# A recurrent (mLSTM) stage rebuilt one chunk ahead of itself, with its gate rows brought by broadcast DMA

## What is computed

```python
def step(carry, inp):
    C, n, m = carry
    qb, kb, vb, li, lf = inp
    bcum = jnp.cumsum(lf, axis=-1)
    dmat = bcum[..., :, None] - bcum[..., None, :] + li[..., None, :]
    dmat = jnp.where(causal, dmat, -jnp.inf)
    inter = bcum + m[..., None]
    m_t = jnp.maximum(inter, jnp.max(dmat, axis=-1))
    w_intra = jnp.exp(dmat - m_t[..., None])
    w_inter = jnp.exp(inter - m_t)
    s_qk = jnp.einsum('bhtd,bhsd->bhts', qb, kb) * w_intra
    num = (w_inter[..., None] * jnp.einsum('bhvd,bhtd->bhtv', C, qb)
           + jnp.einsum('bhts,bhsv->bhtv', s_qk, vb))
    den = w_inter * jnp.einsum('bhd,bhtd->bht', n, qb) + jnp.sum(s_qk, axis=-1)
    h = num / jnp.maximum(jnp.abs(den), jnp.exp(-m_t))[..., None]
    ...
    C_new = decay[..., None, None] * C + jnp.einsum('bhs,bhsv,bhsd->bhvd', w_state, vb, kb)
    ...
```

## Time and profile before

| what | value |
|---|---|
| median of 3 runs | 2396.52 us (2394.82 to 2397.51) |
| the profiled execution | 2397.14 us, its span 2395.4 us |
| TensorE busy | 2280.5 us (95% of the span) |
| VectorE, ScalarE, GpSimd busy | 1256.0, 681.5, 108.7 us |
| mean granted TensorE clock | 0.982 of full |
| recurrent stage on TensorE | first instruction of chunk 0 at 236.00 us, of chunk 7 at 366.11 us |

### The profile page before, as it was taken

The page is one execution under the profiler, slowest core; times in us unless marked ns, Lnnn a source line. Parts: engine busy times, 40 slices in busy tenths (PEclk is TensorE's granted clock), DMA queues, the critical chain, the costliest instruction groups (busy, mean ns, idle before and its releaser), DMA issues. The chain is left out here.

```text
span 2395.4 us, 28953 instructions
## 1 busy us (share of the span) xinstructions
PE 2280.5 (95%) x10838; PEld 1895.0 (79%) x10838; DVE 1256.0 (52%) x2161; ACT 681.5 (28%) x1328; POOL 108.7 (5%) x156
## 2 busy tenths in 40 slices
PE   4999899999999999999998988999999999999997
PEld 3788678787888888888887867987788888888886
DVE  6334443568555455455566546756834433433447
ACT  2300333344112112113145227814411211211221
POOL 0000001110000000000021000011100000000003
PEclk9999899999999999999999998999999999999999
DMA  6433223212332232232221101111211201210211
GB/s 249 124 105 120 92 64 113 71 36 71 91 121 78 89 114 79 87 114 88 82 85 64 50 30 45 37 36 53 71 40 48 70 31 39 70 38 32 70 36 70
DMA packets 48354, 179.77 MB, mean 75 GB/s; under 512 B 6112, under 2 KB 6256, under 8 KB 47760
## 3 DMA queue, kind: packets, MB, share of 16 engines
q1 hardware_dynamic: 42768, 161.50, 21.5%
q0 software_dynamic: 4752, 16.93, 2.0%
q10 hardware_dynamic: 752, 0.22, 0.0%
HBM read 170.24 MB, written 8.39 MB: 75 GB/s over the span
## 5 line engine op out<-in xcount | busy, mean ns | idle before, releaser
L1441 PE MATMUL ps<-uhi,whi 128*128 128x512 f32 x1152 | 452.2, 393 | 15.2 <-DVE ulo L931 7.3
L1442 PE MATMUL ps<-ulo,whi 128*128 128x512 f32 x1152 | 450.3, 391 | 0.0
L1443 PE MATMUL ps<-uhi,wlo 128*128 128x512 f32 x1152 | 450.2, 391 | 0.0
L1441 PE MATMUL ps<-whi,hhi 128*128 128x512 f32 x1024 | 401.1, 392 | 5.2 <-DVE resid L1237 5.2
L1442 PE MATMUL ps<-wlo,hhi 128*128 128x512 f32 x1024 | 399.6, 390 | 0.0
L1443 PE MATMUL ps<-whi,hlo 128*128 128x512 f32 x1024 | 399.5, 390 | 0.0
L1237 DVE TENSOR_TENSOR resid<-ps,resid 128x512 f32<-128x512 f32 x256 | 176.4, 691 | 355.7 <-PE ps L1443 340.0
L733 ACT ACTIVATE h_whole<-ps 128x512 f32<-128x512 f32 x128 | 76.4, 597 | 835.3 <-PE ps L1443 835.3
L1441 PE MATMUL ps<-whi,uhi 128*128 128x512 f32 x704 | 282.7, 402 | 12.4 <-DVE wlo L900 9.0
L900 DVE TENSOR_TENSOR wlo<-stage,whi 128x1024 fp32r<-128x1024 f32 x180 | 219.8, 1225 | 124.4 <-ACT whi L572 124.3
L1443 PE MATMUL ps<-whi,ulo 128*128 128x512 f32 x704 | 277.0, 394 | 0.0
(11 more groups left out here) (214 smaller groups left out, 2149.6 us busy)
## 6 DMA issues: line engine op xcount, KB each, us to landing
stage<-in_stream SPq DMA_DIRECT2D x276, 512.0 KB, 3.6
aux<-in_early SPq DMA_DIRECT2D x2, 2048.0 KB, 10.7
early_place<-in_early SPq DMA_DIRECT2D x2, 2048.0 KB, 19.9
resid<-in_xt SPq DMA_DIRECT2D x8, 512.0 KB, 24.8
resid<-in_x POOLq DMA_DIRECT2D x8, 512.0 KB, 6.7
resid_dram<-resid POOLq DMA_DIRECT2D x8, 512.0 KB, 3.0
resid<-resid_dram POOLq DMA_DIRECT2D x8, 512.0 KB, 3.5
out<-resid SPq DMA_DIRECT2D x8, 512.0 KB, 2.6
```

Source lines behind the costliest of these rows:

```text
L1441: pe.matmul(dst, left_hi, right_hi, start=start, stop=False)
L1442: pe.matmul(dst, left_hi, right_lo, start=False, stop=False)
L1443: return pe.matmul(dst, left_lo, right_hi, start=False, stop=stop)
```

## The change

- The rows of `negm` and `winter` are no longer made by TensorE. GpSimd writes both arrays to DRAM once, then for each chunk issues two DMAs on its own queue that read four rows of 512 bytes and write them to all 128 partitions: `winter` rows into `decay_rows`, `negm` rows straight into `dmat` (256 KB each). ScalarE takes the exp in place from SBUF.
- Scores and transposed keys of chunk c+1 are made at the start of chunk c; those of chunk 0 inside the v pass. `ktok` has two buffers. The weighted scores are written over the keys in `qk`.
- The numerators are made in two pairs of heads, both pairs in banks X+2 and X+3. VectorE copies each pair to `qk` (`take_raw`), so squares and scaling on ScalarE read and write SBUF. Chunk 0 leaves out the products with the zero state.
- The state products use bank M, one head at a time, each waiting for the update of the head before.
- The o projection of chunk c stands in chunk c (parts 0 and 1, then 2, then 3, with the state products between), no longer in chunk c+1.
- On GpSimd the preparation of chunk c+1 stands ahead of the power of chunk c.
- The heads lie in another order in `qk`, so `transpose_tile` reads them `by_pairs`.

```diff
@@ gpsimd
-            for c in range(T):
-
+            pool.wait_ge(gate_v, 11)
+            pool.wait_ge(gate_e, 7)
+            for w, src in enumerate((negm, winter)):
+                pool.dma_start(rows_dram[w], src[:]).then_inc(rows_out, 16)
+            pool.wait_ge(rows_out, 32)
+            def chunk_rows(w, c, dst, landed):
+                src = rows_dram[w].rearrange("(h t) n -> t h n", t=T)[c]
+                pool.dma_start(dst, src.partition_broadcast(P)).then_inc(landed, 16)
+            def prepare(c):
+                if c:
+                    pool.wait_ge(q_weighted, c)
+                chunk_rows(1, c, decay_rows[:].rearrange("p (h n) -> p h n", h=H), winter_in)
+                if c:
+                    pool.wait_ge(s_ready, c)
+                chunk_rows(0, c, dmat[:], negm_in)
                 pool.wait_ge(d_ready, c + 1)
                 pool.affine_select(out=dmat[:], in_=dmat[:], ...
+            prepare(0)
+            for c in range(T):
+                if c + 1 < T:
+                    prepare(c + 1)
                 pool.wait_ge(ms_ready, c + 1)
                 pool.tensor_tensor(mean, mean, neghalf[:], ALU.pow).then_inc(rms_ready, 1)
@@ scalar
+            act.wait_ge(rows_out, 32)
+            decays(0)
+            keys_by_token(0)
+            splits(18, 19)
             for c in range(T):
+                if c + 1 < T:
+                    decays(c + 1)
+                    keys_by_token(c + 1)
+                if c == 0:
+                    splits(20, 21)
                 for h in range(H):
+                    act.wait_ge(raw_ready, 2 * c + h // 2 + 1)
+                    if H * c + h:
+                        act.wait_ge(ss_ready, H * c + h)
+                    act.activation(squares[:], head_out(c, h), ACT.Square,
                                    accum_out=sumsq[:, h:h + 1]).then_inc(ss_ready, 1)
                 act.wait_ge(f_ready, c + 1)
                 for h in range(H):
+                    act.activation(head_out(c, h), head_out(c, h), ACT.Copy,
                                    scale=factor[:, h:h + 1]).then_inc(hs_ready, 1)
+                evac_o(0, c)
@@ vector
+            def take_raw(c, pair):
+                if c:
+                    v.wait_ge(f_ready, c)
+                v.wait_ge(num_done, H * c + 2 * pair + 2)
+                v.tensor_copy(r[:, 2 * pair:2 * pair + 2], ps[:, X + 2:X + 4, DV])
+                v.tensor_copy(two_heads(c, pair), ps[:, X + 2:X + 4, 0:DV]).then_inc(raw_ready, 1)
             for c in range(T):
+                if c + 1 < T:
+                    weigh(c + 1)
+                take_raw(c, 0)
                 if c == 4:
                     take_mod(G_F0)
+                update(c, 0)
+                more = range(2 * (c % 4), 2 * (c % 4) + 2)
+                adas((G_F0, SH_KV)[c // 4], more[0:1] if c else more)
+                if c:
+                    apply_gate(0, c - 1)
+                take_raw(c, 1)
+                update(c, 1)
...
                 v.tensor_scalar(mean, mean, 1.0 / DV, RMS_EPS, ALU.mult, ALU.add).then_inc(ms_ready, 1)
+                update(c, 2)
                 v.wait_ge(rms_ready, c + 1)
                 v.tensor_tensor(factor, mean, r, ALU.mult).then_inc(f_ready, 1)
+                if c == 0:
+                    preps(20, 21)
                 else:
+                    adas((G_F0, SH_KV)[c // 4], more[1:2])
+                update(c, 3)
@@ tensor
             for c in range(T):
+                if c + 1 < T:
+                    scores_and_keys(c + 1)
+                numerators(c, 0)
+                if c == 4:
                     pe.wait_ge(c_updated, H * c)
+                    sum_vector(G_F0)
+                by_token(FIRST["o0"] + c, W_O, c, part=(0, 1))
+                if c == 0:
+                    pe.wait_ge(sum_read, SC_F0 + 1)
+                if c == 4:
+                    pe.wait_ge(sum_read, G_F0 + 1)
+                state(c, 0)
+                numerators(c, 1)
+                state(c, 1)
+                by_token(FIRST["o0"] + c, W_O, c, part=(2,))
+                state(c, 2)
+                by_token(FIRST["o0"] + c, W_O, c, part=(3,))
+                state(c, 3)
+            pe.wait_ge(c_updated, H * (T - 1))
             sum_vector(SH_KV)
-            by_token(FIRST["o0"] + T - 1, W_O, T - 1)
```

More of the change, by code:

```diff
@@ L273, in build @@
         with ExitStack() as a:
+            squares = sb("squares", [P, DV], where=a)
+        with ExitStack() as a:
             rope = sb("rope", [P, T, 2 * ROT], where=a)
@@ L281, in build @@
             dmat = sb("dmat", [P, H, P], where=a)
[L282 to L286, removed]
+            ktok = sb("ktok", [P, 2, H, P], where=a)
+            with ExitStack() as b:
+                gw = sb("gw", [P, K, 8], where=b)
+                gws = sb("gws", [P, K, 16], F32R, where=b)
+                gt = sb("gt", [P, 4, 2 * HC], where=b)
+            decay_rows = sb("decay_rows", [P, H * P], where=a)
         m_prev_col = gt[0:HC, 3, 0:1]
@@ L1059, in _ @@
+            for c in range(T):
+                if c + 1 < T:
+                    weigh(c + 1)
+                take_raw(c, 0)
                 if c == 4:
                     take_mod(G_F0)
[L1061 to L1065 removed]
+                update(c, 0)
[5 more added lines that the diff above has]
+                update(c, 1)
+                v.wait_ge(raw_ready, 2 * c + 2)
@@ L1590, in _, with scores_and_keys @@
             sum_vector(G_M0)
+            def scores_and_keys(c):
+                if c:
+                    pe.wait_ge(s_ready, c)
+                else:
+                    pe.wait_ge(act_evac, 16)
+                for h in range(H):
+                    last = pe.matmul(ps[:, X, h * P:(h + 1) * P], qk[:, c, (H + h) * P:(H + h + 1) * P],
+                                     qk[:, c, h * P:(h + 1) * P], start=True, stop=True)
+                last.then_inc(s_made, 1)
+                if c:
+                    pe.wait_ge(ktok_ready, c)
+                for h in range(H):
+                    last = pe.transpose(ps[:, X + 1, h * P:(h + 1) * P], qk[:, c, (H + h) * P:(H + h + 1) * P],
+                                        ident[:])
+                last.then_inc(k_turned, 1)
             for nh in range(2):
@@ new lines, in _, with numerators @@
+                    if nh == 1 and t == 2:
+                        scores_and_keys(0)
+            pe.wait_ge(dve_evac, 16)
+            sum_vector(SC_F0)
+            def numerators(c, pair):
+                pe.wait_ge(s_ready, c + 1)
+                n = 2 * c + pair
+                if n:
+                    pe.wait_ge(raw_ready, n)
+                for h in (2 * pair, 2 * pair + 1):
+                    val = resid[:, c, h * (DV + 1):(h + 1) * (DV + 1)]
+                    last = pe.matmul(ps[:, X + 2 + h % 2, 0:DV + 1], qk[:, c, (H + h) * P:(H + h + 1) * P], val,
+                                     start=True, stop=(c == 0))
+                    if c:
+                        pe.wait_ge(c_updated, H * (c - 1) + h + 1)
+                        last = pe.matmul(ps[:, X + 2 + h % 2, 0:DV + 1], qk[:, c, h * P:(h + 1) * P],
+                                         cstate[:, h, :], start=False, stop=True)
+                    last.then_inc(num_done, 1)
```

160 lines of the change are left out of this document (65 added, 95 removed).

## The result

The change makes the kernel slower by 0.6%: 2411.62 us (median of 4, 2409.27 to 2414.53) against 2397.02 us for the kernel before on the same chip (median of 4, 2394.82 to 2399.16), a ratio of 1.006 with a 95% interval of 1.0046 to 1.0074. Forecast were 2378.6 us and faster. The profiled execution of the changed kernel has a span of 2407.5 us, against 2395.4.

A forecast was written before the change was run, and what follows sets the result against it. TensorE, busy 95% of the span, bounds the kernel; after the change a 15.2 us loop over chunks binds the stage. 46.6 us saved less 28.7 given back gains 17.9: 2378.6 us against 2396.52, range 2362 to 2394.

The forecast's parts named there:

- the landing L: In the loop over chunks, time from issue to landing of the `negm` row DMA, second of a pair: 4.1 us.
- the wait of 2.4 us: TensorE's idle time per chunk ahead of the second pair of numerators, in chunks 3 to 6: 2.4 us each.
- TensorE's own work: TensorE's work in one chunk of the recurrent stage, without waits and row copies: 12.8 us.
- C: Rival: issue goes by the piece (2.2 us) or each gap drops the clock; loop 17.8 us, kernel 2392 us; chance 0.16.
- D: Rival: slower than before, with issue 2.2 us and landing 6.7 us; loop 20.2 us, kernel 2404 us; chance 0.07.
- the loop: Chain over the chunks through four engines and a DMA queue, from one weighting of scores to the next: 15.2 us.
- Chunk 0's gap: TensorE idle in chunk 0 ahead of the fourth state product, behind weight blocks 20 and 21: about 5.2 us.
- The end: After the last chunks: `sum_vector(SH_KV)` waits 2.5 us, and the o1 pass's last weight block loads 1.5 us later.
- The clock: TensorE's clock behind gaps of 2.4 us in the steady chunks: on the edge, one drop, 1.5 us.
- the mark: Start of the o1 pass, at about 386.2 us before and forecast near 368 us; what it moves, the end moves.
- the 28.7 us given back: New idle time and clock loss on TensorE, 8.3 + 5.5 + 9.4 + 2.5 + 1.5 + 1.5, set against 46.6 us saved.
- B: Rival: rows land early, in 3.2 us with issue 0.55; loop 13.8 us, no clock drop, kernel 2369 us; chance 0.20.

The follow-up runs named there:

- e13: Changed kernel with the heads' rows of a chunk 9 rows (4.5 KB) apart in DRAM in place of 8 (4 KB); 2383.15 us, ratio 0.9947.
- e2: Changed kernel with GpSimd issuing the two row DMAs for chunk c+2 ahead of the power of chunk c; 2370.82 us, ratio 0.9886.
- e11: Measurement in the changed kernel: ten 256 KB broadcasts one at a time in the v pass, five source and piece shapes, twice each; landings 3.2 to 5.5 us.
- e12: Measurement in the changed kernel: ten 256 KB broadcasts one at a time, rows 8, 9, 2, 5 apart and 1 KB pieces 17 apart; landings 3.7 to 6.1 us.
- e1: Changed kernel with each chunk's four rows side by side in DRAM, one 2 KB piece per partition; 2384.84 us, ratio 0.9942.
- e9: Changed kernel with each row transfer in two pieces of 1 KB per partition in place of four of 512 bytes; 2413.7 us, ratio 1.0066.

## Why the prediction was wrong

**The step that failed is the landing L.** "Here a pair of 256 KB follow each other ... 4.1 us, nearer to the pair than to the lone one but with half the bytes": the second of the pair took 8.6 us, over the upper bound of 6.7. All bounds came from DMAs that read a distinct or unbroken source; I reasoned from bytes and, for the issue, from the count of pieces, and never looked at where the rows lie: 4 KB apart, all read by all 128 partitions. e13 changes that one distance and gets the wait of 2.4 us, chunks of 15.6 us on average against 15.2, the o1 pass at 368.70 us against 368.3, and 2383 us against 2378.6. With L right, the sum would have been right to 5 us. In part that is luck: e13's chunks of 16.3 to 16.8 us have a drop of the clock which I had charged once in all, and TensorE's own work, shorter than reckoned, makes up for part of it.

In numbers: five chunks (2 to 6) took 383.9 - 281.4 = 102.5 us instead of 5 x 15.2 = 76, which is 26.5 of the 29.1 us. Of 5.3 us a chunk, 4.5 are the landing and some 1.4 the second pair at half clock, a term that stood in rivals C and D and not in mine; the rest of the loop was a little shorter than reckoned. The other 2.6 us are what is left over in chunks 0, 1 and 7. Chunk 1 is the likely place: I gave it no wait for rows, TensorE waited 4.31 us there, and it lasts 21.5 us where e13 with its early landing has 15.1.

**Right.** The loop, its place on TensorE and its releaser (L1123, behind L1081, the mask, the exps, the DMA), except in chunk 4. The issue at 0.8 us. Row copies gone. Chunk 0's gap, 5.38 for 5.2 us. The end, 2.53 and 1.74 for 2.5 and 1.5 us. The copies on VectorE and in-place scaling at nothing: in e2 TensorE is busy all through chunk 3.

**Off by a little.** TensorE's own work in a chunk is 12.26 us (e2), not 12.8. It changes nothing where the loop is the bound. The clock: I had it drop once in five chunks for gaps of 2.4 us. Gaps of 4.0 to 6.0 us dropped it in every chunk (0.83 or 0.84), and with the gaps of the size forecast, in e13, it fell in three chunks of five (0.90, 0.90, 1.00, 0.90, 1.00). The wait at the start of chunk 0 was 2.02 us for 1.2. And the mark: of the 28.7 us given back, 1.5 lie behind the start of the o1 pass, so my own sum puts it at 366.8 us and not near 368.

**The rivals.** D was the outcome in size (a loop of 20.2 us and 2404 us forecast, 20.5 and 2411.6 measured), with two of its three terms: the half clock, and a landing beyond its 6.7 us; its issue of 2.2 us was wrong. It had a chance of 0.07 because "only the load of eight in a row shows 6.7". That was too little: a landing without a row of its own was half of what the forecast rested on, and with the half clock's 1.2 us in the loop any L above 6.5 us (10.6 + 0.5 + 1.2 + L = 18.8) decided for it, a value inside my own bounds. B is near what the Trainium skill gives (DMA: Bandwidth & Descriptors, Anatomy of one DMA): 2.0 us plus bytes over 436 GB/s, by estimate 2.6 us for 256 KB. The runs disagree: none of the twenty DMAs of 256 KB in e11 and e12 landed in under 3.2 us, and the shape of the change took 4.9 to 5.2 with no other row DMA beside it. The same page of the Trainium skill (Latency and other measured facts) has a row that I could have weighed: an HBM row pitch at a large power of two slows copies (207 GB/s at 512 KiB, 103 at 4 MiB), and 4 KiB of padding restores them where 192 bytes don't. Its pitches are far larger than the 4 KB here, where 512 bytes of padding undid the slow landing (8.6 to 4.8 us); that the cause is the same isn't shown.

## What to carry to other kernels

When a transfer takes the place of computed data, ask first how many steps ahead it is issued, and which in-order engine holds this step's work behind the next step's data: in e2 a landing of 8.7 us left no wait in the loop, in the change one of 8.6 set the length of every chunk. Bytes alone don't price a broadcast, it also counts where its source lies: lay what one transfer reads side by side (e1), or try another distance and measure it (e13), since 8.5 KB with pieces of 1 KB was as dear as 8. And where the largest term of a loop has no row in the trace, its bounds are not bounds; give the other side of the decision point the chance that such ignorance deserves.

## What the runs showed of the hardware that I had not expected

- Four rows of 512 bytes, read by all partitions, take some twice the packet time at a distance of 4 KB (20 to 32 us) that they take at 4.5 KB (13), and in a pair the second lands at 8.6 instead of 4.8 us. Two pieces of 1 KB, 8 or 8.5 KB apart, take 33 to 42 us. Why wasn't found; the number of pieces is not the reason.
- GpSimd's issue takes 0.54 to 0.60 us for one piece per partition (e1) and 0.70 to 0.81 for two or four (e9, e11, the change): more than one piece costs once, and how many hardly counts.
- Such broadcasts hold up the transfers beside them: in the stage a weight load of 512 KB lands in 8.5 us (median) in the change, in 3.8 with the rows 9 apart (e13) and in 3.8 before.
- TensorE's clock after idle time: behind the gaps of 5.38 and 5.95 us shown above two instructions of 257 columns took 1.20 us, twice their 0.60 at full clock. Gaps of 2.36 to 2.83 us were enough too: in e13 the clock fell with the end of the one before 285.69 (0.96 us), and soon behind the one before 302.03 (0.67 us, then 1.06 us at 303.78). Behind a gap of 2.06 us, in e13's chunk 6, it stayed at 1.00. The length of the gap alone doesn't decide: in the kernel before a gap of 2.21 us was followed by the half clock, and behind one of 2.60 us, which ended at 598.78, the clock was 1.00.
